# Three moved pieces of order in a two-block kernel: smaller first weight pieces, a level copy ahead of a split, and the last even unit inside a weight piece

## The reference, cut to what matters

```python
k, v = jnp.split(mem_n @ w_kv, 2, axis=-1)            # first block: w_mem_kv is used first of all weights
...
decay = jnp.exp(jnp.minimum(diff, 0.0)) * tri[:, :, None]
A = jnp.einsum('bhtsd,bhsd->bhts', qc[:, :, :, None, :] * decay, kc)     # second block, per head
o = (jnp.einsum('bhts,bhsv->bhtv', A, vc)
     + jnp.einsum('bhtd,bhdv->bhtv', qc * jnp.exp(b), state))
```

## Time and profile before

| | |
|---|---|
| median of 3 runs | 1035.93 us (1034.16 to 1036.73) |
| the profiled execution | 1035.72 us |
| its span | 1033.9 us |
| PE busy | 1019.1 us, 99% |
| DVE busy | 730.4 us, 71% |
| ACT busy | 654.8 us, 63% |
| granted clock of PE | 0.998 |
| moved by DMA | 167.54 MB, 162 GB/s on average |

### The profile page before, as it was taken

The page is one execution under the profiler, slowest core; times in us unless marked ns, Lnnn a source line. Parts: engine busy times, 40 slices in busy tenths (PEclk is TensorE's granted clock), DMA queues, the critical chain, the costliest instruction groups (busy, mean ns, idle before and its releaser), DMA issues.

```text
span 1033.9 us, 19279 instructions
## 1 busy us (share of the span) xinstructions
PE 1019.1 (99%) x8170; PEld 913.0 (88%) x8170; DVE 730.4 (71%) x1070; ACT 654.8 (63%) x911; POOL 11.3 (1%) x15
## 2 busy tenths in 40 slices
PE   9999999999999999999999999999999999999997
PEld 7899987888989999988999998888799999988875
DVE  5774688875656887765565758977875556598686
ACT  7687667554465565544466678658755667776683
POOL 0000000000000000000000000100000000001000
PEclk9999999999999999999999999999999999999999
DMA  8852444476547556666544533423665455344231
GB/s 293 303 190 82 144 163 150 157 240 203 175 154 235 175 166 197 194 216 187 169 161 120 174 128 122 136 92 104 197 198 161 144 152 164 103 143 144 84 103 62
DMA packets 97430, 167.54 MB, mean 162 GB/s; under 512 B 6912, under 2 KB 32256, under 8 KB 96832
## 3 DMA queue, kind: packets, MB, share of 16 engines
q1 hardware_dynamic: 95792, 159.18, 48.6%
q0 software_dynamic: 1120, 5.51, 1.5%
q10 hardware_dynamic: 432, 1.62, 0.4%
HBM read 165.23 MB, written 1.05 MB: 161 GB/s over the span
## 4 chain that ended last, share of the span: by engine, by line
PE 86%; DVE 5%; ACT 4%; DMA 3%; issue 2%; SPq 0%; DVEq 0%; ACTq 0%
PE proj L634 12%; PE proj L625 12%; PE proj L636 12%; PE proj L635 12%; PE proj L627 12%; PE proj L626 12%; DMA raw<-in_w_in 2%; DVE wlo L1587 2%; ACT whi L1110 1%; PE mix L695 1%; PE mix L987 1%; PE mix L670 1%; DVE arena L532 1%; PE mix L955 1%; PE mix L956 1%
## 5 line engine op out<-in xcount | busy, mean ns | idle before, releaser
L1587 DVE TENSOR_TENSOR wlo<-raw,whi 128x1024 fp32r<-128x1024 f32 (+2 forms) x304 | 355.1, 1199 | 139.7 <-ACT whi L1110 138.2
L1110 ACT ACTIVATE whi<-raw 128x1024 fp32r<-128x1024 f32 (+2 forms) x304 | 305.8, 1038 | 146.4 <-PE proj L636 63.4
L625 PE MATMUL proj<-act_hi,whi 128*128 128x256 f32 x1064 | 303.5, 285 | 0.9 <-ACT arena L1388 0.5
L627 PE MATMUL proj<-act_hi,wlo 128*128 128x256 f32 x1064 | 300.9, 283 | 0.0
L626 PE MATMUL proj<-act_lo,whi 128*128 128x256 f32 x1064 | 300.9, 283 | 0.0
L625 PEld LDWEIGHTS proj<-act_hi,whi 128*128 128x128 f32 x1064 | 203.1, 191 | 3.9 <-ACT arena L1388 1.4
L626 PEld LDWEIGHTS proj<-act_lo,whi 128*128 128x128 f32 x1064 | 203.2, 191 | 0.9
L627 PEld LDWEIGHTS proj<-act_hi,wlo 128*128 128x128 f32 x1064 | 203.2, 191 | 0.2
L634 PE MATMUL proj<-whi,y_hi 128*128 128x512 f32 (+1 forms) x340 | 134.9, 397 | 0.9 <-DVE wlo L1587 0.7
L635 PE MATMUL proj<-wlo,y_hi 128*128 128x512 f32 (+1 forms) x340 | 131.8, 388 | 0.0
L636 PE MATMUL proj<-whi,y_lo 128*128 128x512 f32 (+1 forms) x340 | 131.7, 387 | 0.0
(11 more groups left out here) (360 smaller groups left out, 1233.0 us busy)
## 6 DMA issues: line engine op xcount, KB each, us to landing
raw<-in_w_in SPq DMA_DIRECT2D x144, 512.0 KB, 4.4
raw<-in_w_up SPq DMA_DIRECT2D x88, 256.0 KB, 4.4
raw<-in_w_out SPq DMA_DIRECT2D x32, 512.0 KB, 4.4
raw<-in_w_down SPq DMA_DIRECT2D x22, 512.0 KB, 4.6
raw<-in_w_mem_k SPq DMA_DIRECT2D x8, 512.0 KB, 4.3
raw<-in_w_o SPq DMA_DIRECT2D x8, 512.0 KB, 4.1
raw<-in_w_mem_v SPq DMA_DIRECT2D x8, 512.0 KB, 4.5
raw<-in_w_mem_kv SPq DMA_DIRECT2D x7, 512.0 KB, 6.6
```

What stands on the lines that cost most here:

```text
L625: mm(o, wh[:, i, wc], hi[:, k0 + i, :], start=begin and j % 2 == 0, stop=False, skip_group_check=True)
L627: last = mm(o, wl[:, i, wc], hi[:, k0 + i, :], start=False, stop=end, skip_group_check=True)
L1110: fn(whi[c % SPLIT][:, 0:w], raw[c % SLOTS][:, 0:w], ACT.Copy).then_inc(s.w_hi, 1)
L1587: tt(wlo[c % SPLIT][:, 0:w], raw[c % SLOTS][:, 0:w], f32(whi[c % SPLIT][:, 0:w]), ALU.subtract).then_inc(s.w_lo, 1)
```

## The change

Three edits, each of which moves work and takes none away.

1. `xak` is cut into four pieces of 256 KB and two of 512 KB. There is one piece more, so the points of the order at the start that are written as piece numbers move by one: the third load of the memory now stands behind piece 3, that of `X` behind piece 6, and the splits of ACT and DVE ahead of later steps go one piece further.
2. On DVE, in each layer, one split moves from behind `factors(1)` to behind `factors(0)`, and the other one from ahead of `keep(0)` to behind it.
3. On PE, in each layer, the second half of the decays of unit 7 and `products(6)` move from behind the first piece of `mlaout1` to its middle, between its two halves of tokens.

```diff
-    groups = [("xak", [piece(kv, k * P, 1, 0, 512) for k in range(2)] + wide(kv, 0, row=2 * P, rows=DM - 2 * P)), ("xav", wide(kv, 512))]
+    groups = [("xak", [piece(kv, k * P, 1, 0, 512) for k in range(4)] + wide(kv, 0, row=4 * P, rows=DM - 4 * P)), ("xav", wide(kv, 512))]
...
-                if c == 3:
+                if c == 4:
                     sp.dma_start(MEM[:, 4:8, :], a["mem"][:, 4:8, :]).then_inc(s.mem_rest, 16)
-                if c == SLOTS + 2:
+                if c == SLOTS + 3:
                     sp.dma_start(X[:, :, :], a["x"][0].rearrange("(b p) d -> p b d", p=P)).then_inc(s.x_in, 16)
...
-            def project(name, L, hi, lo, tile0=0, ready=None, part=None, half=None):
+            def project(name, L, hi, lo, tile0=0, ready=None, part=None, half=None, amid=None):
...
                             if half is not None and n == len(ps) - 1 and b == 0:
                                 last.then_inc(half, 1)
+                            if amid is not None and b == 0:
+                                amid()
                     last.then_inc(s.w_used, 1)
...
+                def last_even():
+                    decays(UNITS - 1, 2, 4)
+                    products(UNITS - 2)
+
                 for u in range(1, UNITS):
...
-                        project("mlaout1", L, y_hi, y_lo, 8, part=(0, 1))
-                    decays(u, 2, 4)
+                        project("mlaout1", L, y_hi, y_lo, 8, part=(0, 1), amid=last_even)
+                    if u < UNITS - 1:
+                        decays(u, 2, 4)
...
-                    products(u - 1)
+                    if u < UNITS - 1:
+                        products(u - 1)
...
-            split_until(3)
+            split_until(4)
             act.wait_ge(s.mem_rest, 16)
             mem_upper(range(4, KT))
...
-            split_until(3)
+            split_until(4)
             mem_lower(range(4, KT))
...
                     if u == 0:
-                        split_until(ahead_of("mlaout0", L, 0))
+                        split_until(ahead_of("mlaout0", L, 1))
                     if u == 1:
                         dve.wait_ge(s.hg_zero, L + 1)
-                        split_until(ahead_of("hgi1", L, 3))
                     if u:
                         keep(u - 1)
+                    if u == 1:
+                        split_until(ahead_of("hgi1", L, 3))
```

More of the change, by code:

```diff
@@ L1190, in _ @@
             mem_upper(range(2, 4))
-            split_until(3)
+            split_until(4)
             act.wait_ge(s.mem_rest, 16)
             mem_upper(range(4, KT))
-            split_until(SLOTS + 1)
+            split_until(SLOTS + 2)
             fn(MEM_SQ, MEM, ACT.Square).then_inc(s.mem_sq, 1)
-            split_until(SLOTS + 2)
+            split_until(SLOTS + 3)
             FIRST_SS, FIRST_R = stat[:, 232:234], stat[:, 236:240]
@@ L1201, in _ @@
             link(last)
-            split_until(SLOTS + 3)
+            split_until(SLOTS + 4)
             fn(FIRST_R[:, 2:4], FIRST_SS, ACT.Ln, bias=epsb[:, 0:1], scale=1.0 / DM)
@@ L1670, in _ @@
             tt(MEM_SUM, MEM_SUM, MEM_SQ[:, 1, :], ALU.add).then_inc(s.mem_sum, 1)
-            split_until(SLOTS + 3)
+            split_until(SLOTS + 4)
             norm(0, X, 238)
-            split_until(SLOTS + 5)
+            split_until(SLOTS + 6)
             turned("h", None, KT, act_hi, act_lo, lambda k: cols1[:, 0, k:k + 1]).then_inc(s.mixed, 1)
```

## The result

The changed kernel takes 1037.81 us (median of 14 runs, 1035.77 to 1040.64); the kernel before, on the same chip, 1035.96 us. The ratio is 1.0019 with a 95% interval of 1.0012 to 1.0027: slower by 0.2%, about 2 us. The forecast was 1033.6 us, 2.3 us faster, and the range ended at 1035.3. The profiled execution of the changed kernel took 1039.93 us with a span of 1038.1, 4.2 us over the profiled execution of before, so its trace shows more of the loss than the median has.

A forecast was written before the change was run, and what follows sets the result against it. PE, busy 99% of the span, was taken as the bound, so only its idle time could change. 1035.72 - 2.0 (second edit) - 0.1 (third) + 0 (first) = 1033.6 us, range 1031.9 to 1035.3.

The forecast's parts named there:

- Smaller first pieces: At the start, PE's wait of 0.74 us moves from the third piece to the next one: 0.
- The bound that the forecast kept for this: At the start, +1.8 us if the load issued only after the first split took the median 6.6 us.
- Its rival: The start slips because the piece reusing the first buffer lands late: +1.8 at most, 1033.6 to 1035.4 us; chance 0.08.
- First-pair levels ahead of a split: On DVE, keep(0) directly after factors(1) removes PE's wait ahead of products(1) in both layers: -2.0 us, at most -2.2.
- Last even unit amid a piece: On PE at mlaout1's first piece, idle time filled behind products(6) reopens ahead of it: -0.1 us; ends -0.45 and +1.6.
- the wait for issue: PE's idle time inside products(7) with nothing visible being waited for, 2.1 us in two waits, 0.87 in layer 0.
- the second edit was handed on: Rival: something else holds PE soon behind products(1), giving back up to 2.0 us, 1035.6 us; chance 0.07.
- the supply of instructions: Rival: it bounds the stretch of the units, so the 2.0 us is given back, 1037.3 us; chance 0.05.
- the first rival: The wait for issue goes with the third edit's move and no other replaces it: 1033.0 us; chance 0.14.
- the second: Rival: the start slips because the piece reusing the first buffer lands late, +1.8 us at most; chance 0.08.
- slower by over 0.3%: Whole kernel: the outcome left to the instruction-supply rival at its worst and to unforeseen causes; chance 0.04.

The follow-up runs named there:

- e6: The changed kernel with its third and fourth pieces (256 KB each) side by side in one load buffer; 1037.09 us, 1.0001 of the kernel before.
- e2: The kernel before with the first edit alone; 1040.15 us, 1.0042 of the kernel before.
- e5: The changed kernel with POOL's loads of the tree released by the 17th split in place of the 16th; 1036.32 us, 0.9997 of the kernel before.
- e3: The kernel before with the second edit alone; 1034.42 us, 0.9983 of the kernel before.
- e11: The kernel before with the first edit, the shared load buffer and the tree's release one split later; 1036.21 us, 0.9992 of the kernel before.
- e7: The changed kernel with both repairs, the shared load buffer and the tree's release one split later; 1034.74 us, 0.9979 of the kernel before.
- e8: The kernel before with the tree's release by the 15th split in place of the 16th; 1038.83 us, 1.0022 of the kernel before.
- e13: The kernel before with the second edit alone, a repeat of e3; 1033.96 us, 0.9977 of the kernel before.
- e14: The kernel before with the second edit and the tree's release one split later, a repeat run; 1033.42 us, 0.9972 of the kernel before.

## Why the prediction was wrong

- **Smaller first pieces, taken at 0**: this is the step that failed. "I take 0, because a full queue means that the 6.6 us are time in line, and the line is no longer than before." Whatever the line, SP could not put the loads into it, since each waited for a split: `X` was issued at 10.70 in place of 8.68. e6, which issues them as early again with the same small pieces, has PE at the transposes at 26.46, against 27.78 in the changed kernel and 26.38 before. The DMA rates fit this but do not prove it: in 10 to 15 us 342 GB/s against 398, 308 in e2 and 302 in e5, but 338 in e3 too, which has the start of before and was on time (26.18). The Trainium skill, "DMA: Bandwidth & Descriptors", section Bandwidth, advises to batch transfers to 1 MiB or more, by which the small transfers would be suspect; e11 has the same four transfers of 256 KB and does not lose, so here their size was not the cause. The bound that the forecast kept for this, +1.8 us, came out in size by luck (1.46 in the trace, some 2 us by the ratios of e6 and e7): it was worked out for the piece with tiles 4 and 5, whose first matmul was on time (14.63), and the loss came behind it. Its rival had 0.08.
- **What was not in the sum at all**: the forecast read SP's queue, where the diff moves piece numbers, and has no term for POOL. It did not look for piece numbers that the diff leaves alone. There is one, in POOL's order, and it costs about as much again: +2.3 us in the kernel before (e8), 2.3 us less when mended (e5). In the profiled execution it was 3.15 us of wait and 1.5 us of lower clock.
- **First-pair levels ahead of a split**: right in its mechanism in both layers, and -2.0 stands beside -1.8 and -2.4 us measured (e3, e13).
- **Last even unit amid a piece**: right that PE waits for ACT there (1.36 us, 1.45 forecast), and beside the profiled execution of before the small rest of -0.1 us was met (+0.10 and -0.17 us in the two layers). What was wrong is what there was to gain: the forecast took the 0.87 us of issue in layer 0 for a part of the kernel, and eight of the ten other traces without the edit do not have it. So the term should have been a small loss (0.25 to 0.53 us by pairs of traces, some 0.8 by the ratios). Of the wait for issue nothing was left in any of the seven kernels with the third edit, while the kernel before and all ten kernels without that edit list 0.7 to 2.1 us of it. That the wait goes agrees with the Trainium skill, "Runtime: NRT & Kernel Launch", section Instruction fetch mechanics, by which crossing a block is mostly hidden; that the waits stood at a block's border, no run shows.
- **The rivals**: the second edit was handed on; the supply of instructions did not become the bound; the wait for issue went with the move, as the first rival said, but nothing was gained by it; the start slipped, as the second said, behind the piece that it named, and POOL's queue, which it did not name, cost as much again.
- **The chances**: "slower by over 0.3%" had 0.04, and the kernel came out 0.19% slower, within that bound. The error is in the time and the range, not in that chance.

## What to carry to other kernels

When a change inserts a piece into a numbered stream, search every engine's order for numbers that count that stream, those that the diff leaves alone too; each is a trigger that now fires one piece early. A load that has to wait for a buffer is not "in the queue": to say that a transfer is hidden because the DMA engines are full, show that it is issued before the queue runs low. And count small pieces by the buffers that they occupy: two halves in one buffer cost no place in line.

## What the runs showed of the hardware

```profile
180.00:185.00 5.00, 5.00 (x18) 4.00 (x18) 2.49 (x8) 4.97 (x5) 0.00 (x0) 0.74 0.71 246
```

```profile
180.00:185.00 5.00, 5.00 (x26) 4.22 (x25) 2.50 (x6) 4.97 (x6) 0.00 (x0) 1.00 0.60 220
```

  Four runs of e14 lie at 1032.5 to 1033.6 us with a mean clock of 0.998, two at 1034.7 with 0.997, so executions of one kernel are 1 to 2 us apart with the clock. What sets it was not tried.
- In the stretch from 60 to 65 us, around PE's wait of 3.0 us, the clock was 0.81, and 0.84 in the 5 us behind; around one of 3.1 us (e8) 0.86 and 0.80; with a wait of 1.3 us (e6) it was 1.00.
- The DMA share was 1.00 at 342 GB/s (the changed kernel), 1.01 at 338 (e3) and 1.05 at 398, each over 10 to 15 us: a share of 1 does not say how much is moved.
